# Projection stage of a decoder step: the gated channels' squares are summed before one product with ones, and that product goes ahead of k's turning

## The chip, the cores and the metric

The kernel runs on one core of a Trainium2 chip. The metric is the device time of one execution in microseconds (us); lower is better. The time of the kernel before is the median of three runs.

## The reference, cut to what matters

One decoder layer over a prompt of 2048 tokens (width 1024) and a small group of 32 sample tokens. The part that the change touches is the prompt's mixed projection and the recurrent branch:

```python
xn = rms_norm(x, p['norm_mix']) * (1 + scale1) + shift1
proj = xn @ p['w_in']
q, k, v, xr, yb = jnp.split(proj, [W_ATTN, 2 * W_ATTN, 3 * W_ATTN, 3 * W_ATTN + W_RG], axis=-1)
...
xc, conv_new = causal_conv(xr, conv_buf, p['conv_w'], p['conv_b'])
h, h_last = rg_lru(xc, h0, p['rg_wa'], p['rg_ba'], p['rg_wx'], p['rg_bx'], p['rg_lambda'])
rg = rms_norm(h * jax.nn.gelu(yb), p['norm_rg'])
```

The last line is the one that matters: for each token, the mean over the 512 gated channels of the square of h times gelu(yb), its root, and the division by it. Attention, the output projection, the routed experts and the final norm follow and are not touched.

## The kernel before, in words

The program is a series of stages, each in a block of its own with a barrier of all engines behind it: modulation, projection of the prompt (`projection_phase`), projection of the samples (`sample_projection_phase`), attention, router, experts, final norm. Everything is float32.

`projection_phase` works through the prompt in four groups of 512 tokens (`NGRP` is 4, `GRP` 512). A group's results lie with channels on the 128 partitions and tokens along the row, except v and k, whose rows are tokens (four tiles of 128 tokens, `TPG`). PSUM has eight banks of 128x512 float32, and each bank's filling is a job. `JOBS` (from L293) lists the 41 jobs of a group in order, with the engine that empties each bank: xT0 to xT7 (x turned, emptied by VectorE, DVE), xr, yb (four each, ScalarE, ACT), q (DVE), r, i (the two gates, ACT), v (ACT), k (DVE), kT (k turned, four jobs, DVE), and last rms (ACT).

TensorE (PE, L394 to L442) runs a group's jobs in that order. `free_bank` (L397) waits until the bank's last job has been emptied. Job n of a group takes bank n modulo 8, counted from 0 anew in each group. So xT0 of a group takes bank 0, which rms, job 40 of the group before, has filled: xT0 waits until ACT has emptied rms. A 128x128 transposition turns one piece (L410 for x, L439 for k), and `product` (L413, L418) accumulates matrix products into a bank. After k's last product PE waits until DVE has copied the fourth tile of k (k3) out of its bank (L435), turns k in 16 pieces, all pieces of a channel block before the next block, then waits for the squares (L441) and multiplies them by a matrix of ones, four products that add up in one bank (L442). That sums the squares over the 128 partitions and over the four channel blocks.

ACT (L445 to L503) empties xr, yb, r, i and v, takes sigmoids, exponentials and roots, normalises x of the next group (`norm`, L448), squares the gated channels (L501) once DVE has made them (L568), and takes the root of rms (L503) into `rrow`.

DVE (L506 to L577) empties xT with scale and shift (L528), finishes the group before (`finish`, L515: reciprocal of `rrow`, L518, and four multiplications, L521), does the convolution (L539, L541), copies q (L548), prepares the recurrence and scans (L563), multiplies by the gate (L568), copies k's four tiles into `k_st` (L571) and the turned k into `qk_st` (L575). In the last group `finish` follows these copies directly (L577).

SyncE (SP, L366 to L391) loads the next group's x and stores q, v, k, kT and the normed channels rgT (L380, L387) in this order, then waits until all have landed. The stage after begins when every engine has passed the barrier.

Of the kernel before, what the change touches and what calls it, by code (L numbers as in the profile page):

```python
# [11 lines left out]
ALU = mybir.AluOpType  # L12
ACT = mybir.ActivationFunctionType
AX_X = mybir.AxisListType.X

P = 128
# [84 lines left out]
def modulation_phase(nc, io, keep, sems):  # L101
# [3 lines left out]
    with ExitStack() as stack:  # L105
# [198 lines left out]
def emptied(n, engine):  # L304

    return sum(e == engine for _, e in JOBS[:n + 1])


def projection_phase(nc, io, keep, sems):
# [3 lines left out]
    with ExitStack() as stack:  # L313
# [21 lines left out]
        s_xc, s_ga, s_th, s_m2, s_m, s_sig, s_gp, s_gy, s_rg, s_rq, s_rt, s_rgn = (  # L335
            k.sem(f"p2_{n}") for n in ("xc", "ga", "th", "m2", "m", "sig", "gp", "gy", "rg", "rq", "rt", "rgn"))
        st_q, st_v, st_k, st_kT, st_rg, s_stored = (
            k.sem(f"p2_st_{n}") for n in ("q", "v", "k", "kT", "rg", "all"))
        ident, ones, vecT, modT, w_in = (keep[n] for n in ("ident", "ones", "vecT", "modT", "w_in"))
# [23 lines left out]
        with nc.Block() as block:  # L363
# [29 lines left out]
            @block.tensor  # L393
            def _(pe):  # L394
                for g in range(NGRP):

                    def free_bank(n):  # L397

                        before = [m for m in range(NJ) if m % 8 == n % 8]
                        at = before.index(n)  # L400
                        m = before[at - 1]
                        e = JOBS[m][1]
                        pe.wait_ge(out_sem[e], (g + (1 if at else 0)) * n_of[e] + emptied(m, e))
                        return bank[n % 8]

                    pe.wait_ge(s_xn, g + 1)
                    for c in range(KC):
                        ps = free_bank(JOB[f"xT{c}"])
                        for j in range(TPG):
                            mm = pe.transpose(ps[:, j * P:j * P + P], x_t[:, j, c * P:c * P + P], ident[:, :])  # L410
                        mm.then_inc(made, 1)

                    def product(name, parts):  # L413
                        ps = free_bank(JOB[name])
                        for i, (w, m) in enumerate(parts):
                            if name == "xr0":
                                wait_out(pe, f"xT{i}", g)
                            mm = pe.matmul(ps[:, :], w, m, start=(i == 0), stop=(i == len(parts) - 1))  # L418
                        mm.then_inc(made, 1)

                    for part in ("xr", "yb", "q"):
                        pe.wait_ge(sems[f"w_{part}"], 16)
                        for f in range(FC):
                            at = wcol[part] + f * P
                            product(f"{part}{f}", [(w_in[:, c, at:at + P], xnT[:, c, :]) for c in range(KC)])
                    pe.wait_ge(s_xc, g + 1)
                    for n, part in enumerate(("r", "i")):
                        for f in range(FC):
                            product(f"{part}{f}", [(keep["w_gate"][:, n, f, :], xc[:, f, :])])
                    for part in ("v", "k"):  # L430
                        pe.wait_ge(sems[f"w_{part}"], 16)
                        at = wcol[part]
                        for j in range(TPG):
                            product(f"{part}{j}", [(xnT[:, c, j * P:j * P + P], w_in[:, c, at:at + WA]) for c in range(KC)])
                    wait_out(pe, f"k{TPG - 1}", g)  # L435
                    for f in range(FC):
                        ps = free_bank(JOB[f"kT{f}"])
                        for j in range(TPG):
                            mm = pe.transpose(ps[:, j * P:j * P + P], k_st[:, j, f * P:f * P + P], ident[:, :])  # L439
                        mm.then_inc(made, 1)  # L440
                    pe.wait_ge(s_rq, g + 1)  # L441
                    product("rms", [(ones[:, :], gt[:, f, :]) for f in range(FC)])  # L442

            @block.scalar
            def _(act):  # L445
# [18 lines left out]
                for g in range(NGRP):  # L464
                    for f in range(FC):
                        wait_made(act, f"xr{f}", g)
                        act.activation(xr[:, f, CONV - 1:], bank[JOB[f"xr{f}"] % 8][:, :], ACT.Copy).then_inc(act_out, 1)
                    for f in range(FC):
                        wait_made(act, f"yb{f}", g)
                        act.activation(yb[:, f, :], bank[JOB[f"yb{f}"] % 8][:, :], ACT.Copy).then_inc(act_out, 1)  # L470
                    act.wait_ge(s_gp, g + 1)
                    act.activation(gt[:, :, :], gt[:, :, :], ACT.Sigmoid, scale=GELU_OUT).then_inc(s_sig, 1)
                    for f in range(FC):
                        wait_made(act, f"r{f}", g)
                        act.activation(ra[:, f, :], bank[JOB[f"r{f}"] % 8][:, :], ACT.Sigmoid, bias=vcol("rg_ba", f)).then_inc(act_out, 1)
                    for f in range(FC):
                        wait_made(act, f"i{f}", g)
                        act.activation(ig[:, f, :], bank[JOB[f"i{f}"] % 8][:, :], ACT.Sigmoid, bias=vcol("rg_bx", f)).then_inc(act_out, 1)
                    act.wait_ge(s_stored, g + 1)
                    act.drain()  # L480
                    for f in range(FC):
                        act.activation(th[:, f, :], ra[:, f, :], ACT.Tanh, scale=keep["coef"][:, f:f + 1])
                    act.drain()
                    for f in range(FC):
                        last = act.activation(ra[:, f, :], ra[:, f, :], ACT.Exp, scale=keep["coef"][:, f:f + 1])
                    act.drain().then_inc(s_th, 1)

                    def values(first, last):
                        for j in range(first, last):
                            wait_made(act, f"v{j}", g)  # L490
                            act.activation(v_st[:, j, :], bank[JOB[f"v{j}"] % 8][:, :], ACT.Copy).then_inc(act_out, 1)
# [11 lines left out]
                    act.activation(rrow[:, :], bank[JOB["rms"] % 8][:, :], ACT.Sqrt, bias=keep["eps"][:, 0:1]).then_inc(act_out, 1)  # L503

            @block.vector
            def _(dve):  # L506
# [18 lines left out]
                for g in range(NGRP):  # L525
                    for c in range(KC):
                        wait_made(dve, f"xT{c}", g)
                        dve.tensor_scalar(xnT[:, c, :], bank[JOB[f"xT{c}"] % 8][:, :], keep["A1T"][:, c, 0:1],  # L528
                                          modT[:, SHIFT1 + c, 0:1], ALU.mult, ALU.add).then_inc(dve_out, 1)
                    if g:  # L530
                        finish(g - 1)
# [13 lines left out]
                    dve.wait_ge(s_stored, g + 1)  # L545
                    for f in range(FC):
                        wait_made(dve, f"q{f}", g)
                        dve.tensor_copy(qk_st[:, f, :], bank[JOB[f"q{f}"] % 8][:, :]).then_inc(dve_out, 1)  # L548
# [18 lines left out]
                    dve.wait_ge(s_gy, g + 1)  # L567
                    dve.tensor_tensor(hs[:, :, :], hs[:, :, :], yb[:, :, :], ALU.mult).then_inc(s_rg, 1)  # L568
                    for j in range(TPG):
                        wait_made(dve, f"k{j}", g)  # L570
                        dve.tensor_copy(k_st[:, j, :], bank[JOB[f"k{j}"] % 8][:, :]).then_inc(dve_out, 1)  # L571
                    dve.wait_ge(st_q, 16 * g + 16)
                    for f in range(FC):
                        wait_made(dve, f"kT{f}", g)
                        dve.tensor_copy(qk_st[:, f, :], bank[JOB[f"kT{f}"] % 8][:, :]).then_inc(dve_out, 1)  # L575

                finish(NGRP - 1)  # L577

# [1618 lines left out]
```

## Time and profile before

| | |
|---|---|
| median of three runs | 2992.24 us (2990.52 to 2995.51) |
| the profiled execution's own time | 2991.91 us |
| its span in the trace | 2990.2 us |
| mean granted TensorE clock | 0.962 of full speed |
| TensorE busy | 2739.4 us, 92% of the span |
| VectorE busy | 1347.6 us, 45% |
| ScalarE busy | 963.5 us, 32% |
| GpSimd busy | 471.7 us, 16% |

Busy time of an engine says that an instruction of it was running, not that it ran at its peak. A float32 product of 128x128 by 128x512 is two records in the trace ("passes" below); a transposition is one. Row lines give the start, the length, the engine, the source line, and in brackets how long the engine sat idle before and what ended that. PEld is TensorE's loading of weights, which runs beside its products. The projection of the prompt spans from 40 us to about 674 us of the trace.

### The profile page before, as it was taken

The numbers are of one execution on the slowest core, as the hardware profiler recorded it, in microseconds if no ns is written. First come the engines' busy times: TensorE is split into PE (matmuls) and PEld (weight loads), VectorE is DVE, ScalarE is ACT, GpSimd is POOL, SyncE is SP. The second block draws the span as 40 slices with busy tenths as digits, with TensorE's granted clock in tenths as the row PEclk, the third lists the DMA queues.
The fourth block names the chain that finished last, engine by engine and source line by source line (L and its number), as shares of the span: only waits on it lengthen the run. The fifth ranks groups of instructions, "written<-read, shape, count | busy, mean of one in ns | idle before, by whom it ended". The sixth has DMA issues, their size and how long they took to land. (4 is left out here: it accounts for less than half of the span.)

```text
span 2990.2 us, 45603 instructions
## 1 busy us (share of the span) xinstructions
PE 2739.4 (92%) x15137; PEld 1363.8 (46%) x15137; DVE 1347.6 (45%) x2726; ACT 963.5 (32%) x1858; POOL 471.7 (16%) x669
## 2 busy tenths in 40 slices
PE   7999999986899898899999999399999998999978
PEld 3444444432444444444444555255555554455533
DVE  2231414132778687778786777212212221122218
ACT  2222222121777677677771221110001010010004
POOL 0101010101011111121110222211111111111123
PEclk8999999997999999999999999699999999999989
DMA  8020201018586767676664433586896479968737
GB/s 316 14 84 14 74 25 56 14 56 310 160 275 203 265 200 246 205 249 204 230 217 153 148 131 117 204 273 218 288 302 216 149 235 354 351 218 271 241 100 315
DMA packets 275921, 575.74 MB, mean 193 GB/s; under 512 B 59270, under 2 KB 75719, under 8 KB 271740
## 3 DMA queue, kind: packets, MB, share of 16 engines
q1 hardware_dynamic: 192936, 427.99, 41.4%
q0 software_dynamic: 82480, 145.43, 15.3%
q8 instruction: 89, 1.46, 0.2%
q14 instruction: 92, 0.75, 0.1%
q10 hardware_dynamic: 324, 0.10, 0.0%
HBM read 460.86 MB, written 112.29 MB: 192 GB/s over the span
## 5 line engine op out<-in xcount | busy, mean ns | idle before, releaser
L1930 PE MATMUL h<-w,xT 128*64 128x256 f32 x5120 | 589.0, 383 | 22.2 <-DMA w<-in_w 18.1
L1930 PEld LDWEIGHTS h<-w,xT 128*64 128x64 f32 x5120 | 362.7, 138 | 244.6 <-issue 75.2
L1220 DVE TENSOR_TENSOR_SCAN left<-leave,left 128x512 f32<-128x512 f32 (+3 forms) x320 | 358.7, 1121 | 159.0 <-ACT leave L1102 157.9
L418 PE MATMUL bank<-xnT,w_in 128*128 128x512 f32 x768 | 330.3, 592 | 0.0
L1943 PE MATMUL yb<-w,hT 128*64 128x512 f32 x1280 | 309.4, 604 | 0.0
L1911 ACT ACTIVATE sg<-h 128x128 f32<-128x128 f32 x160 | 44.3, 277 | 692.1 <-PE h L1930 692.1
L1023 POOL DMA_DIRECT2D w_out<-in_cache_v x256 | 137.4, 537 | 689.2 <-issue 687.6
L1589 PE MATMUL pb<-w_out,featT 128*128 128x512 f32 x512 | 227.7, 597 | 2.2 <-DVE t L1654 2.2
L418 PEld LDWEIGHTS bank<-xnT,w_in 128*128 128x128 f32 x768 | 145.6, 190 | 181.8 <-issue 180.6
L1976 DVE TENSOR_TENSOR sg<-sg,h 128x128 f32<-128x128 f32 x160 | 46.1, 288 | 388.0 <-ACT sg L1911 388.0
L418 PE MATMUL bank<-w_in,xnT 128*128 128x512 f32 x512 | 220.4, 592 | 0.0
L1271 PE MATMUL tb<-ident,take 128*128 128x128 f32 x1088 | 188.1, 289 | 23.0 <-DVE take L1126 18.4
L1102 ACT ACTIVATE leave<-zb,nbiasP 128x512 f32<-128x512 f32 (+3 forms) x320 | 203.6, 636 | 7.9 <-PE zb L1264 7.9
L1104 ACT ACTIVATE take<-zb,biasP 128x512 f32<-128x512 f32 (+3 forms) x320 | 206.1, 644 | 0.0
L1126 DVE TENSOR_TENSOR take<-take,left 128x512 f32<-128x512 f32 (+3 forms) x320 | 194.8, 609 | 15.8 <-DVE left L1220 0.4
L1271 PEld LDWEIGHTS tb<-ident,take 128*128 128x128 f32 x1088 | 117.1, 143 | 167.3 <-issue 108.6
L1258 PE MATMUL zb<-w 64*128 64x512 f32 (+3 forms) x640 | 164.4, 591 | 30.3 <-ACT take L1104 18.7
L1304 PE MATMUL tb<-ident,w_out 128*128 128x128 f32 x1024 | 159.9, 280 | 31.7 <-DMA w_out<-in_cache_k 23.2
L1291 PE MATMUL ob<-wT,vv 128*64 128x256 f32 (+1 forms) x1152 | 183.3, 398 | 1.7 <-ACT wT L1034 1.6
L1034 ACT ACTIVATE wT<-tb 128x512 f32<-128x512 f32 (+3 forms) x240 | 130.9, 545 | 102.1 <-PE tb L1271 101.1
L418 PEld LDWEIGHTS bank<-w_in,xnT 128*128 128x128 f32 x512 | 97.3, 190 | 122.5 <-issue 122.5
L1885 POOL DMA_DIRECT2D ys_d<-y x82 | 70.2, 857 | 501.3 <-DMA ys_d<-y 408.1
(372 smaller groups left out, 2873.9 us busy)
## 6 DMA issues: line engine op xcount, KB each, us to landing
w<-in_w SPq DMA_DIRECT2D x96, 2048.0 KB, 23.8
w_out<-in_cache_v POOLq DMA_DIRECT2D x256, 256.0 KB, 5.0
w_out<-in_cache_k SPq DMA_DIRECT2D x256, 256.0 KB, 3.9
ys_d<-zeros SPq DMA_DIRECT2D x32, 816.0 KB
slab<-in_w_ada SPq DMA_DIRECT2D x24, 1024.0 KB, 17.9
ys_d<-y POOLq DMA_DIRECT2D x83, 256.0 KB, 9.8
x_in<-xs_d POOLq DMA_DIRECT2D x162, 128.0 KB, 6.3
w_in<-in_w_in SPq DMA_DIRECT2D x5, 2048.0 KB, 20.3
```

The source lines that it names most:

```text
L418: mm = pe.matmul(ps[:, :], w, m, start=(i == 0), stop=(i == len(parts) - 1))
L1102: act.activation(leave[n % 4][:, 0:cols], zb[n % 3][:, 0:cols], ACT.Sigmoid, scale=-SCALE, bias=keep["nbiasP"][:, head:head + 1]).then_inc ...
L1104: act.activation(take[n % 4][:, 0:cols], zb[n % 3][:, 0:cols], ACT.Sigmoid, scale=SCALE, bias=keep["biasP"][:, head:head + 1]).then_inc(s_ ...
L1126: dve.tensor_tensor(take[n % 4][:, 0:cols], take[n % 4][:, 0:cols], left[n % 4][:, 1:cols + 1], ALU.mult).then_inc(s_w, 1)
L1220: dve.tensor_tensor_scan(left[n % 4][:, 0:cols][:, ::-1], leave[n % 4][:, 0:cols][:, ::-1], leave[n % 4][:, 0:cols][:, ::-1], left[n % 4][ ...
L1258: mm = pe.matmul(zb[(n + par) % 3][:, 0:cols], qT[pair % 2][half, t * P:t * P + P], kT[pair % 2][half, c * GRP:c * GRP + cols], start=True ...
L1271: mm = pe.transpose(to[:, j * P:j * P + P], take[n % 4][:, j * P:j * P + P], ident[:, :])
L1291: mm = pe.matmul(o[64 * par:64 * par + 64, q0:2 * P], vv[pair % 2][:, c * TPG + j, 64 * par:64 * par + 64], wT[m % 2][par][:, j, :, :].rea ...
L1304: mm = pe.transpose(to[:, i * P:i * P + P], kp[g % 2][:, i, f * P:f * P + P], ident[:, :])
L1589: mm = pe.matmul(pb[half][0:n, :], lhs, w_out[:, half, c, :], start=(c == 0), stop=(c == KC - 1))
L1930: mm = pe.matmul(h[half][q * G:q * G + G, 0:2 * P], xT[:, c % (XW // P), c // (XW // P) * G:c // (XW // P) * G + G], w13[i][:, c, :, cols] ...
L1943: mm = pe.matmul(yb[p * G:p * G + G, :], hT[:, half, q * G:q * G + G], w2[i][:, q * (EC // STRIPS) + half, p * XW:p * XW + XW], start=(hal ...
```

## The change

It has three parts. First, once DVE has copied k2 and before it copies k3, it waits for the squares and adds them up over the four channel blocks with two additions (128x1024, then 128x512); PE then makes one product with ones in place of four. Second, the job rms moves ahead of kT, so PE makes this product right behind k's products, and turns k piece by piece in the order of its tiles: all four banks of kT are claimed first, and each token tile's four pieces wait only for that tile's copy. Third, banks are counted on through the groups: the job's number over the whole stage modulo 8 names the bank, and `free_bank` waits for the job eight places before. The helper `at` gives the bank to ACT and DVE.

```diff
-        [(f"kT{f}", "dve") for f in range(FC)] + [("rms", "act")])
+        [("rms", "act")] + [(f"kT{f}", "dve") for f in range(FC)])
...
+        def at(name, g):
+
+            return bank[(g * NJ + JOB[name]) % 8]
...
-                    def free_bank(n):
-
-                        before = [m for m in range(NJ) if m % 8 == n % 8]
-                        at = before.index(n)
-                        m = before[at - 1]
-                        e = JOBS[m][1]
-                        pe.wait_ge(out_sem[e], (g + (1 if at else 0)) * n_of[e] + emptied(m, e))
-                        return bank[n % 8]
+                    def free_bank(name):
+
+                        n = g * NJ + JOB[name]
+                        if n >= 8:
+                            of, m = divmod(n - 8, NJ)
+                            e = JOBS[m][1]
+                            pe.wait_ge(out_sem[e], (of + 1) * n_of[e] + emptied(m, e))
+                        return at(name, g)
...
-                    wait_out(pe, f"k{TPG - 1}", g)
-                    for f in range(FC):
-                        ps = free_bank(JOB[f"kT{f}"])
-                        for j in range(TPG):
-                            mm = pe.transpose(ps[:, j * P:j * P + P], k_st[:, j, f * P:f * P + P], ident[:, :])
-                        mm.then_inc(made, 1)
-                    pe.wait_ge(s_rq, g + 1)
-                    product("rms", [(ones[:, :], gt[:, f, :]) for f in range(FC)])
+                    pe.wait_ge(s_sum, g + 1)
+                    product("rms", [(ones[:, :], gt[:, 0, :])])
+                    kT = [free_bank(f"kT{f}") for f in range(FC)]
+                    for j in range(TPG):
+                        wait_out(pe, f"k{j}", g)
+                        for f in range(FC):
+                            mm = pe.transpose(kT[f][:, j * P:j * P + P], k_st[:, j, f * P:f * P + P], ident[:, :])
+                            if j == TPG - 1:
+                                mm.then_inc(made, 1)
...
                     for j in range(TPG):
+                        if j == TPG - 1:
+                            dve.wait_ge(s_rq, g + 1)
+                            dve.tensor_tensor(gt[:, 0:2, :], gt[:, 0:2, :], gt[:, 2:4, :], ALU.add)
+                            dve.drain()
+                            dve.tensor_tensor(gt[:, 0, :], gt[:, 0, :], gt[:, 1, :], ALU.add).then_inc(s_sum, 1)
                         wait_made(dve, f"k{j}", g)
-                        dve.tensor_copy(k_st[:, j, :], bank[JOB[f"k{j}"] % 8][:, :]).then_inc(dve_out, 1)
+                        dve.tensor_copy(k_st[:, j, :], at(f"k{j}", g)[:, :]).then_inc(dve_out, 1)
```

The remaining lines of the diff put `at(name, g)` where a bank was named by `bank[JOB[name] % 8]`, and add the semaphore.

## Rows read from the trace of the kernel before

**Rows 1.** Busy time by stretch: us, then busy (instructions) of PE, PEld, DVE, ACT, POOL, clock, DMA.

```profile
100.00:190.00 90.00, 89.81 (x210) 39.48 (x208) 21.53 (x19) 32.00 (x40) 14.52 (x4) 1.00 0.06 23
...
200.00:345.00 145.00, 144.75 (x342) 64.04 (x339) 41.54 (x46) 36.17 (x47) 14.50 (x4) 1.00 0.10 37
```

**Rows 2.** Timeline of the joint between the first group and the second.

```profile
183.64 6.17 PE L418 MATMUL bank<-w_in,xnT 128*128 128x512 f32 x14
...
189.85 0.69 DVE L571 COPY k_st<-bank 128x512 f32<-128x512 f32 x1 [6.17 <-PE bank L418]
...
190.59 1.73 PEld L439 LDWEIGHTS bank<-ident,k_st 128*128 128x128 f32 x16 [1.61 <-DVE k_st L571]
190.59 1.97 PE L439 MATMUL bank<-ident,k_st 128*128 128x128 f32 x16 [0.78 <-DVE k_st L571]
191.36 2.48 DVE L575 COPY qk_st<-bank 128x512 f32<-128x512 f32 x4 [0.82 <-PE bank L439]
...
192.40 3.60 PE L418 MATMUL bank<-gt,ones 128*128 128x512 f32 x8
```

**Rows 3.** Timeline of the same joint, its second half, by engine (ACT, PE, DVE).

```profile
196.03 0.69 ACT L503 ACTIVATE rrow<-bank,eps 128x512 f32<-128x512 f32 x1 [19.49 <-PE bank L418]
...
196.87 3.69 PE L410 MATMUL bank<-ident,x_t 128*128 128x128 f32 x32 [0.87 <-ACT rrow L503]
200.39 15.19 PE L418 MATMUL bank<-xnT,w_in 128*128 128x512 f32 x35
...
197.53 5.84 DVE L528 TENSOR_SCALAR xnT<-bank,A1T,modT 128x512 f32<-128x512 f32 x8 [3.69 <-PE bank L410]
```

**Rows 4.** Timeline of the two later joints: k3's copy in the second and third group.

```profile
344.79 0.69 DVE L571 COPY k_st<-bank 128x512 f32<-128x512 f32 x1 [6.17 <-PE bank L418]
...
499.73 0.69 DVE L571 COPY k_st<-bank 128x512 f32<-128x512 f32 x1 [6.18 <-PE bank L418]
```

**Rows 5.** Timeline of DVE ahead of k3's copy in the first group, and of ACT.

```profile
172.31 2.29 DVE L568 TENSOR_TENSOR th<-th,yb 128x2048 f32<-128x2048 f32 x1
...
182.98 0.69 DVE L571 COPY k_st<-bank 128x512 f32<-128x512 f32 x1 [6.17 <-PE bank L418]
...
174.63 1.91 ACT L501 ACTIVATE gt<-th 128x2048 f32<-128x2048 f32 x1 [9.86 <-DVE th L568]
```

**Rows 6.** Additions and products of two tensors on DVE elsewhere, shapes apart: busy us, mean ns.

```profile
L1659 DVE TENSOR_TENSOR x<-t,x_t 128x512 f32<-128x512 f32 x32 | 22.2, 693 | 3.0
...
L1673 DVE TENSOR_TENSOR xn<-xn,rowsP 128x1024 f32<-128x1024 f32 x16 | 19.6, 1226 | 1.2
```

**Rows 7.** Timeline of the stage's end and of the next stage's start.

```profile
654.67 0.69 DVE L571 COPY k_st<-bank 128x512 f32<-128x512 f32 x1 [6.17 <-PE bank L418]
...
658.69 0.37 SPq L380 DMA_DIRECT2D kT_d<-qk_st  x1
...
661.57 3.35 DVE L518 RECIPROCAL rrow<-rrow 128x512 f32<-128x512 f32 x1 [2.91 <-ACT rrow L503]
...
667.80 0.37 SPq L387 DMA_DIRECT2D rgT_d<-th  x1
673.60 24.32 SPq L640 DMA_DIRECT2D slab<-in_w_ada  x14
```

**Rows 8.** Clock and DMA in short stretches (columns as in rows 1).

```profile
42.00:43.00 1.00, 1.00 (x7) 1.00 (x6) 0.91 (x3) 0.00 (x0) 0.00 (x0) 0.50 1.04 385
43.00:44.00 1.00, 1.00 (x7) 1.00 (x6) 0.96 (x2) 0.00 (x0) 0.00 (x0) 0.56 1.11 401
44.00:45.00 1.00, 1.00 (x11) 1.00 (x10) 1.00 (x2) 0.00 (x0) 0.00 (x0) 1.00 0.99 362
...
662.00:663.00 1.00, 0.00 (x0) 0.00 (x0) 1.00 (x1) 0.00 (x0) 0.00 (x0) 1.00 0.34 127
...
678.00:679.00 1.00, 1.00 (x12) 0.26 (x8) 0.00 (x0) 0.00 (x0) 0.11 (x1) 0.62 1.03 377
...
660.82:673.64 12.82, 0.00 (x1) 0.04 (x2) 6.10 (x6) 0.69 (x1) 0.00 (x0) 0.67 0.34 127
699.60:709.80 10.20, 9.37 (x48) 4.46 (x44) 0.69 (x1) 2.74 (x13) 0.00 (x0) 0.52 1.01 418
```

**Rows 9.** Timeline of PE at the stage's start, the first group's transpositions of x.

```profile
36.17 1.11 PE L226 MATMUL ps_f<-ident,mod_rows 128*128 128x128 f32 x4
40.07 5.54 PE L410 MATMUL bank<-ident,x_t 128*128 128x128 f32 x32 [2.79 <-ACTq L463]
```

More of the change, by code:

```diff
@@ L334, in projection_phase @@
         s_x, s_xn, s_rs, s_sq = (k.sem(f"p2_{n}") for n in ("x", "xn", "rs", "sq"))
-        s_xc, s_ga, s_th, s_m2, s_m, s_sig, s_gp, s_gy, s_rg, s_rq, s_rt, s_rgn = (
-            k.sem(f"p2_{n}") for n in ("xc", "ga", "th", "m2", "m", "sig", "gp", "gy", "rg", "rq", "rt", "rgn"))
+        s_xc, s_ga, s_th, s_m2, s_m, s_sig, s_gp, s_gy, s_rg, s_rq, s_rt, s_sum, s_rgn = (
+            k.sem(f"p2_{n}") for n in ("xc", "ga", "th", "m2", "m", "sig", "gp", "gy", "rg", "rq", "rt", "sum", "rgn"))
         st_q, st_v, st_k, st_kT, st_rg, s_stored = (
@@ L395, in _ @@
                 for g in range(NGRP):
-                    def free_bank(n):
-                        before = [m for m in range(NJ) if m % 8 == n % 8]
-                        at = before.index(n)
-                        m = before[at - 1]
-                        e = JOBS[m][1]
-                        pe.wait_ge(out_sem[e], (g + (1 if at else 0)) * n_of[e] + emptied(m, e))
-                        return bank[n % 8]
+                    def free_bank(name):
[5 more added lines that the diff above has]
+                        return at(name, g)
                     pe.wait_ge(s_xn, g + 1)
                     for c in range(KC):
-                        ps = free_bank(JOB[f"xT{c}"])
+                        ps = free_bank(f"xT{c}")
                         for j in range(TPG):
@@ L413, in product @@
                     def product(name, parts):
-                        ps = free_bank(JOB[name])
+                        ps = free_bank(name)
                         for i, (w, m) in enumerate(parts):
@@ L423, in _ @@
                         for f in range(FC):
-                            at = wcol[part] + f * P
-                            product(f"{part}{f}", [(w_in[:, c, at:at + P], xnT[:, c, :]) for c in range(KC)])
+                            of = wcol[part] + f * P
+                            product(f"{part}{f}", [(w_in[:, c, of:of + P], xnT[:, c, :]) for c in range(KC)])
                     pe.wait_ge(s_xc, g + 1)
@@ L431, in _ @@
                         pe.wait_ge(sems[f"w_{part}"], 16)
-                        at = wcol[part]
+                        of = wcol[part]
                         for j in range(TPG):
-                            product(f"{part}{j}", [(xnT[:, c, j * P:j * P + P], w_in[:, c, at:at + WA]) for c in range(KC)])
-                    wait_out(pe, f"k{TPG - 1}", g)
-                    for f in range(FC):
-                        ps = free_bank(JOB[f"kT{f}"])
-                        for j in range(TPG):
-                            mm = pe.transpose(ps[:, j * P:j * P + P], k_st[:, j, f * P:f * P + P], ident[:, :])
-                        mm.then_inc(made, 1)
-                    pe.wait_ge(s_rq, g + 1)
-                    product("rms", [(ones[:, :], gt[:, f, :]) for f in range(FC)])
+                            product(f"{part}{j}", [(xnT[:, c, j * P:j * P + P], w_in[:, c, of:of + WA]) for c in range(KC)])
+                    pe.wait_ge(s_sum, g + 1)
[7 more added lines that the diff above has]
+                                mm.then_inc(made, 1)
             @block.scalar
@@ L466, in _ @@
                         wait_made(act, f"xr{f}", g)
-                        act.activation(xr[:, f, CONV - 1:], bank[JOB[f"xr{f}"] % 8][:, :], ACT.Copy).then_inc(act_out, 1)
+                        act.activation(xr[:, f, CONV - 1:], at(f"xr{f}", g)[:, :], ACT.Copy).then_inc(act_out, 1)
                     for f in range(FC):
                         wait_made(act, f"yb{f}", g)
-                        act.activation(yb[:, f, :], bank[JOB[f"yb{f}"] % 8][:, :], ACT.Copy).then_inc(act_out, 1)
+                        act.activation(yb[:, f, :], at(f"yb{f}", g)[:, :], ACT.Copy).then_inc(act_out, 1)
                     act.wait_ge(s_gp, g + 1)
@@ L474, in _ @@
                         wait_made(act, f"r{f}", g)
-                        act.activation(ra[:, f, :], bank[JOB[f"r{f}"] % 8][:, :], ACT.Sigmoid, bias=vcol("rg_ba", f)).then_inc(act_out, 1)
+                        act.activation(ra[:, f, :], at(f"r{f}", g)[:, :], ACT.Sigmoid, bias=vcol("rg_ba", f)).then_inc(act_out, 1)
                     for f in range(FC):
                         wait_made(act, f"i{f}", g)
-                        act.activation(ig[:, f, :], bank[JOB[f"i{f}"] % 8][:, :], ACT.Sigmoid, bias=vcol("rg_bx", f)).then_inc(act_out, 1)
+                        act.activation(ig[:, f, :], at(f"i{f}", g)[:, :], ACT.Sigmoid, bias=vcol("rg_bx", f)).then_inc(act_out, 1)
                     act.wait_ge(s_stored, g + 1)
@@ L490, in values @@
                             wait_made(act, f"v{j}", g)
-                            act.activation(v_st[:, j, :], bank[JOB[f"v{j}"] % 8][:, :], ACT.Copy).then_inc(act_out, 1)
+                            act.activation(v_st[:, j, :], at(f"v{j}", g)[:, :], ACT.Copy).then_inc(act_out, 1)
                     values(0, 2)
@@ L502, in _ @@
                     wait_made(act, "rms", g)
-                    act.activation(rrow[:, :], bank[JOB["rms"] % 8][:, :], ACT.Sqrt, bias=keep["eps"][:, 0:1]).then_inc(act_out, 1)
+                    act.activation(rrow[:, :], at("rms", g)[:, :], ACT.Sqrt, bias=keep["eps"][:, 0:1]).then_inc(act_out, 1)
             @block.vector
@@ L527, in _ @@
                         wait_made(dve, f"xT{c}", g)
-                        dve.tensor_scalar(xnT[:, c, :], bank[JOB[f"xT{c}"] % 8][:, :], keep["A1T"][:, c, 0:1],
+                        dve.tensor_scalar(xnT[:, c, :], at(f"xT{c}", g)[:, :], keep["A1T"][:, c, 0:1],
                                           modT[:, SHIFT1 + c, 0:1], ALU.mult, ALU.add).then_inc(dve_out, 1)
@@ L547, in _ @@
                         wait_made(dve, f"q{f}", g)
-                        dve.tensor_copy(qk_st[:, f, :], bank[JOB[f"q{f}"] % 8][:, :]).then_inc(dve_out, 1)
+                        dve.tensor_copy(qk_st[:, f, :], at(f"q{f}", g)[:, :]).then_inc(dve_out, 1)
                     dve.wait_ge(s_th, g + 1)
@@ L574, in _ @@
                         wait_made(dve, f"kT{f}", g)
-                        dve.tensor_copy(qk_st[:, f, :], bank[JOB[f"kT{f}"] % 8][:, :]).then_inc(dve_out, 1)
+                        dve.tensor_copy(qk_st[:, f, :], at(f"kT{f}", g)[:, :]).then_inc(dve_out, 1)
                 finish(NGRP - 1)
```

## The prediction, made before the changed kernel ran

> **What bounds the kernel now.** I read first the busy time by stretch for the stage that the change touches. Between a group's start and its end TensorE is busy for 89.81 of 90 us and for 144.75 of 145, and no other engine for more than 42 [rows 1]. So inside a group TensorE alone sets the time, and a wait of another engine is free. Next I read the timeline where two groups meet, because only there PE stands still. Its last 14 passes of k's products start at 183.64 and take 6.17 us; one pass lasts 0.592, so the step from pass to pass is (6.17 - 0.592) / 13 = 0.429, the last starts at 189.22 and another could have started at 189.65 [rows 2]. It starts nothing until 190.59: it waits for DVE's copy of k3. Then come 16 transpositions in 1.81 us (to 192.40), then eight passes with ones, the last at 192.40 + 7 x 0.429 = 195.40, so that the next instruction could have started at 195.83. It starts at 196.87, after ACT's root has emptied the rms bank, and x's 32 transpositions take 3.52 us, to 200.39 [rows 3]. The joint thus takes 7.22 us from 189.65 to 196.87: 0.94 of waiting, 1.81 of turning, 3.43 of ones, 1.04 of waiting. The same copy of k3 comes at 344.79 and 499.73, 154.94 after the one before each time [rows 4], so the three joints are alike and a group is a fixed sum of PE's work.
>
> **Part one, four products become one.** PE makes two passes with ones instead of eight: 6 x 0.429 = 2.57 us less in each of the three joints, all on the path. DVE gets two additions. The trace has two-tensor operations of both shapes elsewhere, 1.226 us for 128x1024 and 0.693 for 128x512 [rows 6]; with a drain of some 0.1 that is 2.0 us. They stand between k2's copy, which ends at 183.67, and k3's, for which DVE now waits 6.17 us until 189.85 [rows 2, 5]. Their input is ready: ACT's squares end at 174.63 + 1.91 = 176.54 [rows 5]. So the sum is ready near 185.7, PE asks for it at 189.65, and DVE is back 4.1 us before k3 is made. Cost: nothing, hidden behind k3's products. Were that cover gone, 2.0 us a group would come onto the path. What is queued behind the new wait on DVE is k3's copy, and behind that kT's and the stores of k and kT on SP; the wait has been over for 7 us when DVE comes to it.
>
> **Part two, rms ahead of kT.** The two passes start at 189.65 and 190.08, and the transpositions can start at 190.51. k3's copy ends at 190.54. The pieces of k0 to k2 need nothing of it; they are 12 at 1.73 / 16 = 0.108, so the first piece of k3 starts near 191.81, 1.27 us after that copy. The wait of 0.94 is gone. What is late next is DVE: the four banks of kT are now finished together instead of one after the other. The first copy of kT started 0.77 after the first of its four transpositions, so 0.45 after the last [rows 2]; I put it at 191.81 + 0.45 = 192.26. Four copies take 2.48, to 194.74. ACT's root runs from about 190.7 to 191.4, beside the turning.
>
> **Part three, banks counted on.** xT0 to xT2 now wait for k1 to k3, xT3 for rms, xT4 to xT7 for kT0 to kT3. The first three have long been empty when x's transpositions start at 190.51 + 1.81 = 192.32. xT3 starts 12 pieces later, near 193.6, and needs the root's end at 191.4. xT4 to xT7 start near 194.1, 194.5, 195.0 and 195.4, and need the copies that end near 192.9, 193.6, 194.2 and 194.74. The margin never falls below 0.6 us. The wait of 1.04 is gone. x's transpositions end at 195.84, where xr0's first product needs the first copy of xT: DVE starts it after kT3 at about 194.8, it takes 0.8, done 195.6. That leaves 0.2 us. After that DVE makes a copy each (5.84 - 0.80) / 7 = 0.72 us [rows 3] and PE needs one each two passes, 0.86, so the margin grows. Were all four banks held up by kT's copies, the most that this could cost is their whole 2.48 us.
>
> The joint becomes 0.86 + 1.81 = 2.67 us in place of 7.22: 4.55 less, three times, **13.65 us**.
>
> **The stage's end.** Here DVE and the stores set the end. k3's copy starts at 654.67; DVE starts its reciprocal at 661.57, 6.90 later, because the root comes last; the store of rgT is issued at 667.80 and the next stage starts at 673.60 [rows 7]. Afterwards the root is done 1.5 us behind k3's product, and DVE goes into the reciprocal when its kT copies are done: 2.41 + 2.48 + 0.05 = 4.95 behind k3's copy. All that follows moves up by 6.90 - 4.95 = **1.95 us**. SP's order is kept: k's store where it was, kT's issued 0.9 later than now (4.9 in place of 4.02 behind 654.67), rgT's 1.95 earlier. kT's traffic ends now during 662 to 663 [rows 8], so it would end near 663.2 of the same scale, before rgT's issue at 665.85: they don't meet. In the other joints the same stores lie beside 145 us of PE's work and cost nothing.
>
> **The sum.** 13.65 + 1.95 = 15.6 us less than the profiled execution's own 2991.91: 2976.3. The median of the three runs is 0.33 above that execution, so I forecast **2976.5 us** for the median. Later stages start behind a barrier and move as one piece; I put their change at zero, with 2 to 3 us either way, since the three runs before spread over 5.0 us without any change.
>
> **A rule that speaks against the change.** The change puts k's 16 and x's 32 transpositions side by side, 5.3 us without a product, where now at most 3.5 us of turning stand together with a wait of 1.04 in front. What the trace shows is this: ahead of the stage PE stood still until 40.07, at the lower level of 1.2 GHz (0.50), and then ran transpositions alone [rows 9]. During 43 to 44, still within them, the granted clock began to rise, and from 44 to 45 it was 1.00 [rows 8]. So transpositions have raised the clock, and I expect them to hold it. The Trainium skill, TensorE: Matmul & The Clock Gate, Part 4 (PE-mode transpose), says that transpositions don't count as PE being busy in the same way and don't bring the full clock. By that rule the joint could fall to half speed, which is the second rival below; the trace does not agree with it.
>
> **Rivals.**
> (a) The joint keeps a wait: DVE's kT copies, now bunched, hold up xT4 or the first product. For it: only 0.2 us of margin at the first product. Against: the margins worked out above. Between 0.3 and 2.48 us a joint: 2977.4 to 2983.9; I take 2980 for the case. Chance 0.10.
> (b) The clock falls at the joints. At the next stage's start PE ran at half speed from 673.64 until about 678.6, 5 us [rows 7, 8]; half of that is lost, 2.5 us a joint, 7.5 in all: 2984.0. Against: rows 8 and 9. Chance 0.04.
> (c) A later stage gives some back. The sample projection waits for its weights' transfers, which start behind the barrier and so move with it; but attention and the experts have stretches in which clock and transfers fall differently from run to run. Up to 5 us either way on top: 2971 to 2982. Chance 0.06.
> (d) Slower than before: the clock falls in the joints and stays down. The longest stretch at half speed with PE at work is 10.2 us, 699.6 to 709.8 at 0.52 [rows 8]; that loses 5.1 us a joint, 15.3 in all, and cancels the gain (2991.6). From 5.2 us lost per joint it turns into a loss, and beyond 0.2% it needs 7.2, over 14 us at half speed behind each joint. With 20 us, 10 lost each: 2976.3 + 30 = 3006. No stretch of dense products shows this. Chance 0.01.
> (e) The change doesn't do what it says: the additions are not ready or the passes not fewer. Six passes fewer follow from the text; the squares have 7 us of slack. Were DVE's additions late by over 4 us, PE would stand still ahead of rms with all turning behind it. Each microsecond beyond costs one a joint: 2980 to 2990. Chance 0.01.
>
> **How the numbers follow.** The forecast has 0.78, its own range 2973.5 to 2979.5. About 0.2% of the time, 6 us, is what a measurement of this kernel can tell from no change, so faster means below 2986.3. Forecast, (a), (b) and (c) lie there: 0.78 + 0.10 + 0.04 + 0.06 = 0.98. I keep 0.95 for faster, 0.03 for within 0.2% and 0.02 for slower, since the later stages scatter and (b) could be dearer. The range 2972.5 to 2982.5 holds the forecast and nearly all of (a) and (c).
>
> **What would show each step.** Behind k3's last pass two passes with ones follow at once, then 16 and 32 transpositions without a gap, then xr0: 6.2 us from 189.65 to the first product instead of 10.74. DVE shows two additions of 1.2 and 0.7 us that end about 4 us before k3's copy, then a wait of about 4.1 in place of 6.17. DVE waits some 1.7 us before the first kT copy and hardly at all before x's. k3's copies stand 150.4 apart. The clock stays at 1.00 in the joints. The next stage starts 15.6 us earlier, near 658.0. The forecast is wrong if a gap over 0.3 us is left in the joint, if the granted clock shows 0.50 there, or if the span from the next stage's start to the end differs from now by more than 3 us.

## The result, and the profile after

The changed kernel's median is 2977.32 us over six runs (2973.08 to 2984.49), against 2993.61 (2990.52 to 2997.86) for the kernel before on the same chips. The ratio is 0.9947 with a 95% interval of 0.9931 to 0.9963: 16.3 us less, by medians. The forecast was 2976.5. That the two lie only 0.8 us apart is partly luck: two later medians of the same kernel are 2973.9 and 2972.2. What doesn't depend on luck is the stage's own time, read below from the trace. The profiled execution took 2973.08 us, with a span of 2971.2.

The timeline of the first joint, changed kernel:

```profile
183.16 0.69 DVE L581 COPY k_st<-bank 128x512 f32<-128x512 f32 x1 [6.18 <-PE bank L422]
183.77 1.22 DVE L577 TENSOR_TENSOR gt<-gt 128x1024 f32<-128x1024 f32 x1
185.06 0.69 DVE L579 TENSOR_TENSOR gt<-gt 128x512 f32<-128x512 f32 x1
189.83 1.02 PE L422 MATMUL bank<-gt,ones 128*128 128x512 f32 x2
190.03 0.69 DVE L581 COPY k_st<-bank 128x512 f32<-128x512 f32 x1 [4.28 <-PE bank L422]
190.69 1.91 PE L445 MATMUL bank<-ident,k_st 128*128 128x128 f32 x16
...
190.89 0.69 ACT L508 ACTIVATE rrow<-bank,eps 128x512 f32<-128x512 f32 x1 [14.16 <-PE bank L422]
...
192.38 2.48 DVE L585 COPY qk_st<-bank 128x512 f32<-128x512 f32 x4 [1.66 <-PE bank L445]
192.43 3.66 PE L414 MATMUL bank<-ident,x_t 128*128 128x128 f32 x32
194.78 5.83 DVE L533 TENSOR_SCALAR xnT<-bank,A1T,modT 128x512 f32<-128x512 f32 x8
...
195.93 7.46 PE L422 MATMUL bank<-xnT,w_in 128*128 128x512 f32 x17
```

PE has no bracket any more: two passes with ones from 189.83, k's pieces from 190.69, x's from 192.43, the first product at 195.93. That is 6.10 us from the point where k's products leave PE free to the next group's first product, in place of 10.74 [rows 2, 3]. The additions sit in DVE's old wait, of which the part behind them is left: it shrinks from 6.17 to 4.28 us. k3's copy follows its product at once, as before.

Busy time by stretch (columns as in rows 1) says the same for the later joints: PE doesn't stand still in them.

```profile
340.00:490.00 150.00, 150.00 (x386) 69.22 (x385) 48.70 (x55) 36.87 (x48) 14.53 (x4) 1.00 0.13 49
490.00:640.00 150.00, 150.00 (x387) 69.35 (x386) 48.43 (x54) 28.05 (x35) 14.52 (x4) 1.00 0.09 35
```

The timeline of the stage's end, changed kernel, to be held against [rows 7]:

```profile
640.93 0.69 DVE L581 COPY k_st<-bank 128x512 f32<-128x512 f32 x1 [4.28 <-PE bank L422]
...
643.28 2.48 DVE L585 COPY qk_st<-bank 128x512 f32<-128x512 f32 x4 [1.65 <-PE bank L445]
645.68 3.34 DVE L523 RECIPROCAL rrow<-rrow 128x512 f32<-128x512 f32 x1
645.79 0.37 SPq L384 DMA_DIRECT2D kT_d<-qk_st  x1
...
651.89 0.37 SPq L391 DMA_DIRECT2D rgT_d<-th  x1
657.71 28.99 SPq L650 DMA_DIRECT2D slab<-in_w_ada  x16
```

k3's copies now stand (640.93 - 190.03) / 3 = 150.30 us apart, against 154.94: 4.64 less for each joint. From the last such copy to the next stage it is 16.78 us instead of 18.93: 2.15 less. From the first k3 copy to the next stage, the measure used below, it went from 483.75 us to 467.68: **16.07 less**, 3 x 4.64 + 2.15. The next stage to the end took 2316.6 us before and 2313.5 in this execution, 3.1 less, which the section on the prediction comes back to.

### The profile page after: what moved, and what is told of

Same layout as the page of the kernel before. It is cut to its first block and busy times, and to the rows that moved or that the text cites. A ratio compares the mean times of both kernels' runs of the same rounds, so it can differ in the third digit from the quotient of the medians.

```text
span 2971.2 us, 45570 instructions
## 1 busy us (share of the span) xinstructions
PE 2728.3 (92%) x15113; PEld 1361.5 (46%) x15113; DVE 1355.1 (46%) x2734; ACT 964.4 (32%) x1858; POOL 475.6 (16%) x669
```

## The experiments

The whole time scatters by several us from run to run, far more than the parts to be told apart. So each experiment is read from its trace by positions within the stage: the distance between k3's copies (one group), the stretch from the last of them to the next stage's start (the stage's end), and the whole from the first k3 copy. None of them depends on when the stage began, and that turned out to be needed: the first k3 copy came anywhere from 188.24 to 190.36 us. Each of the first six experiments is a single execution. How well these positions repeat can be seen from the changed kernel, which was profiled three times: 467.68, 467.68 and 467.66 us over the whole stretch.

| kernel | distance of k3's copies | last k3 copy to next stage | first k3 copy to next stage |
|---|---|---|---|
| before | 154.94 | 18.93 | 483.75 |
| changed | 150.30 | 16.78 | 467.68 |
| four products, new order and banks | 152.88 | 19.35 | 477.98 |
| additions alone, old order and banks | 152.37 | 16.38 | 473.48 |
| changed, banks counted anew | 154.57, 152.90, 154.50 | 16.78 | 478.75 |
| changed, k turned by blocks | 150.51 | 16.00 | 467.53 |
| changed, additions behind k3's copy | 153.25 | 21.12 | 480.87 |
| changed, k turned eight times | 162.53 | 29.01 | 516.59 |
| changed, ACT copies kT | 150.30 | 13.62 | 464.52 |

### Four products in the new place

```diff
-                            dve.wait_ge(s_rq, g + 1)
-                            dve.tensor_tensor(gt[:, 0:2, :], gt[:, 0:2, :], gt[:, 2:4, :], ALU.add)
-                            dve.drain()
-                            dve.tensor_tensor(gt[:, 0, :], gt[:, 0, :], gt[:, 1, :], ALU.add).then_inc(s_sum, 1)
...
-                    pe.wait_ge(s_sum, g + 1)
-                    product("rms", [(ones[:, :], gt[:, 0, :])])
+                    pe.wait_ge(s_rq, g + 1)
+                    product("rms", [(ones[:, :], gt[:, f, :]) for f in range(FC)])
```

> The changed kernel without the two additions: rms goes ahead of kT with four products as before. Read by where the next stage (sample projection) starts, 657.71 us in the changed kernel and 673.60 before, and by the distance between k3's copies, 150.30 and 154.94. Theory (the saved passes count fully, the order alone gives only the two waits): six passes of 0.43 come back in every joint, distance 152.9, and the same 2.6 at the stage's end, next stage at 668.0. Rival (the gain is the order's; the passes with ones would lie in time in which PE waited anyway, for instance for k3's copy): distance 150.3 to 151.2, next stage below 662.

Measured: distance 152.88, next stage at 666.49; the stage had begun 1.5 us early (first k3 copy 188.51), and over the stretch it is 10.30 us more than the changed kernel, 2.58 for each of the four groups. The timeline of its first joint:

```profile
188.31 3.60 PE L422 MATMUL bank<-gt,ones 128*128 128x512 f32 x8
188.51 0.69 DVE L576 COPY k_st<-bank 128x512 f32<-128x512 f32 x1 [6.18 <-PE bank L422]
...
191.74 1.91 PE L445 MATMUL bank<-ident,k_st 128*128 128x128 f32 x16
```

The six passes lie fully on the path, and the saved passes were 10.3 of the 16.1 us. The new order and the banks alone bring the other 483.75 - 477.98 = 5.77: about 6.2 in the three joints (154.94 - 152.88 = 2.06 each), less 0.42 at the stage's end, which takes 19.35 us here and took 18.93 before. In the new order the product with ones goes first, so k's pieces and DVE's copies of kT come later, and the reciprocal stands behind them.

### The additions alone, in the kernel before

```diff
                     for j in range(TPG):
+                        if j == TPG - 1:
+                            dve.wait_ge(s_rq, g + 1)
+                            dve.tensor_tensor(gt[:, 0:2, :], gt[:, 0:2, :], gt[:, 2:4, :], ALU.add)
+                            dve.drain()
+                            dve.tensor_tensor(gt[:, 0, :], gt[:, 0, :], gt[:, 1, :], ALU.add).then_inc(s_sum, 1)
...
-                    pe.wait_ge(s_rq, g + 1)
-                    product("rms", [(ones[:, :], gt[:, f, :]) for f in range(FC)])
+                    pe.wait_ge(s_sum, g + 1)
+                    product("rms", [(ones[:, :], gt[:, 0, :])])
```

> The kernel before with the two additions and one product alone; the order kT then rms and the banks stay. Theory: 2.57 us less in each joint, distance of k3's copies 152.4, both waits (0.94 for k3's copy, 1.04 for the root) unchanged; the root at the stage's end 2.57 earlier, next stage at 663.3 to 663.5. Rival (DVE's additions cost something on the way, by k3's copy coming late): k3's copy later than its product, distance above 152.6, next stage later than 664.

Measured: distance 152.37, next stage at 663.71, which is 0.2 later than expected because the first k3 copy came 0.38 later (190.23). Both waits are still there, as the timeline of its first joint shows:

```profile
190.98 1.97 PE L439 MATMUL bank<-ident,k_st 128*128 128x128 f32 x16 [0.79 <-DVE k_st L576]
...
192.78 1.02 PE L418 MATMUL bank<-gt,ones 128*128 128x512 f32 x2
...
194.68 3.69 PE L410 MATMUL bank<-ident,x_t 128*128 128x128 f32 x32 [0.87 <-ACT rrow L503]
```

The additions with the one product are worth 10.27 us by themselves. With the 5.77 of the experiment before this makes 16.04 of the 16.07 measured: the two parts simply add up. They also divide the stage's end: the saved passes alone bring it from 18.93 to 16.38, and the new order takes back 0.40 of that.

### Banks counted anew in each group

```diff
-            return bank[(g * NJ + JOB[name]) % 8]
+            return bank[JOB[name] % 8]
...
-                        n = g * NJ + JOB[name]
-                        if n >= 8:
-                            of, m = divmod(n - 8, NJ)
-                            e = JOBS[m][1]
-                            pe.wait_ge(out_sem[e], (of + 1) * n_of[e] + emptied(m, e))
+                        n = JOB[name]
+                        same = [m for m in range(NJ) if m % 8 == n % 8]
+                        i = same.index(n)
+                        m = same[i - 1]
+                        e = JOBS[m][1]
+                        pe.wait_ge(out_sem[e], (g + (1 if i else 0)) * n_of[e] + emptied(m, e))
```

> The changed kernel, but each group counts its banks from 0 anew, so that xT0 shares a bank with kT3 of the group before. Theory: x's first transposition waits for the copy of kT3, which ends near 194.86 in the first joint in place of a start at 192.43; 2.4 to 2.6 us more in each of three joints, none at the stage's end; distance 152.8, next stage near 665.1. Rival (DVE, which copies kT and then xT, is what paces the joint anyway, so the banks don't matter): distance 150.3 to 151, next stage below 660.

Measured: 154.57, 152.90 and 154.50. Only the middle one is what was expected. The wait is there in all three, 2.41 us until kT3 is copied; what differs is the time that x's 32 transpositions take behind it. The timeline of the first, second and third joint:

```profile
194.59 5.14 PEld L415 LDWEIGHTS bank<-ident,x_t 128*128 128x128 f32 x32 [2.62 <-issue]
194.62 5.35 PE L415 MATMUL bank<-ident,x_t 128*128 128x128 f32 x32 [2.41 <-DVE qk_st L586]
...
349.15 3.48 PEld L415 LDWEIGHTS bank<-ident,x_t 128*128 128x128 f32 x32 [2.62 <-issue]
349.18 3.69 PE L415 MATMUL bank<-ident,x_t 128*128 128x128 f32 x32 [2.41 <-DVE qk_st L586]
...
502.05 5.08 PEld L415 LDWEIGHTS bank<-ident,x_t 128*128 128x128 f32 x32 [2.62 <-issue]
```

and the clock in the first joint, in half microseconds (columns as in rows 1):

```profile
194.50:195.00 0.50, 0.38 (x3) 0.41 (x4) 0.00 (x0) 0.00 (x0) 0.00 (x0) 0.78 0.00 0
195.00:195.50 0.50, 0.50 (x4) 0.50 (x3) 0.00 (x0) 0.00 (x0) 0.00 (x0) 0.50 0.19 74
...
198.50:199.00 0.50, 0.50 (x7) 0.50 (x6) 0.50 (x2) 0.00 (x0) 0.00 (x0) 1.00 0.00 0
```

In two joints of three the granted clock fell to 0.50 (1.2 GHz) as PE came out of the wait, and the transpositions took 1.6 us more until it rose. So banks that restart cost 2.6 us a joint, and 4.2 to 4.3 where the clock falls: 11.07 in all, more than two thirds of what the change brings. With 478.75 us this kernel is 5.27 slower over the stretch than the one with the additions alone (473.48), and would be 2.0 slower without the clock's fall. The reordering pays only together with the banks that count on. The other half of this question was not run: banks that count on in the old order. By the jobs' list xT0 would then share its bank with k1, and rms's bank would go to xT7, so they could remove the wait for the root without any reordering; how the 2.06 us a joint divide between order and banks is open.

### k turned by blocks

```diff
-                    for j in range(TPG):
-                        wait_out(pe, f"k{j}", g)
-                        for f in range(FC):
-                            mm = pe.transpose(kT[f][:, j * P:j * P + P], k_st[:, j, f * P:f * P + P], ident[:, :])
-                            if j == TPG - 1:
-                                mm.then_inc(made, 1)
+                    wait_out(pe, f"k{TPG - 1}", g)
+                    for f in range(FC):
+                        for j in range(TPG):
+                            mm = pe.transpose(kT[f][:, j * P:j * P + P], k_st[:, j, f * P:f * P + P], ident[:, :])
+                        mm.then_inc(made, 1)
```

> The changed kernel, but k is turned block by block after k3's copy, as before, not tile by tile. Theory (rms's two passes already cover k3's copy; the turning by pieces saves nothing more in the joints and makes kT0 later): the first transposition 0.05 to 0.1 later, distance 150.3 to 150.4; DVE's first kT copy 0.8 earlier, and with it the stage's end: next stage at 656.9 to 657.3. Rival (the pieces cover a wait): distance 151 or more, next stage at 659 or later.

Measured: distance 150.51, so 0.21 us a joint, twice the most that I had put; and at the end 16.00 instead of 16.78, since the first copy of kT starts 0.8 earlier. Over the stretch 467.53 against 467.68. The pieces cover 0.2 us of k3's copy in each joint and give it back at the stage's end. Turning by pieces is thus worth nothing in this stage (0.15 us against it); the two passes with ones in front of it do most of the covering.

### The additions behind k3's copy

```diff
                         dve.tensor_copy(k_st[:, j, :], at(f"k{j}", g)[:, :]).then_inc(dve_out, 1)
+                    dve.wait_ge(s_rq, g + 1)
+                    dve.tensor_tensor(gt[:, 0:2, :], gt[:, 0:2, :], gt[:, 2:4, :], ALU.add)
+                    dve.drain()
+                    dve.tensor_tensor(gt[:, 0, :], gt[:, 0, :], gt[:, 1, :], ALU.add).then_inc(s_sum, 1)
```

(and the same four lines taken away ahead of it)

> The changed kernel with the two additions behind k3's copy instead of ahead of it, so that nothing covers them. Theory (the additions are free only because DVE waits for k3's product): the sum is ready 2.0 us behind k3's copy, PE's product with ones starts near 192.8 in place of 189.83 in the first joint, 2.9 to 3.0 us more in each joint and at the stage's end: distance 153.3, next stage near 669.5. Rival (PE has other slack there): less than 1.5 us more a joint.

Measured: distance 153.25, 2.95 more a joint, as expected. The stage's end grew by 4.34 instead of 2.95. The timeline of the first joint and of the last group's end:

```profile
192.66 1.12 PE L422 MATMUL bank<-gt,ones 128*128 128x512 f32 x2 [2.68 <-DVE gt L580]
...
652.40 2.07 PE L422 MATMUL bank<-gt,ones 128*128 128x512 f32 x2 [2.68 <-DVE gt L580]
654.27 2.41 PE L445 MATMUL bank<-ident,k_st 128*128 128x128 f32 x16
...
656.46 2.48 DVE L584 COPY qk_st<-bank 128x512 f32<-128x512 f32 x4 [4.11 <-PE bank L445]
```

and the clock at the last group's end (columns as in rows 1):

```profile
651.50:652.00 0.50, 0.00 (x0) 0.00 (x0) 0.43 (x2) 0.00 (x0) 0.00 (x0) 0.86 0.98 381
652.00:652.50 0.50, 0.10 (x1) 0.10 (x1) 0.35 (x1) 0.00 (x0) 0.00 (x0) 0.50 1.00 389
```

In the three joints ahead of it the same wait of 2.68 us left the clock at 1.00 and the two passes took 1.12 or 1.13. At the last group's end the clock fell during the wait; the two passes took 2.07, and k's turning 2.41 instead of 1.91. DVE's first kT copy starts 4.06 us behind the product with ones there, against 2.65 in the first joint (195.31 behind 192.66). That is the missing 1.4 us.

### k turned eight times over

```diff
+                    for again in range(8):
-                    for j in range(TPG):
+                        for j in range(TPG):
...
-                            if j == TPG - 1:
+                                if j == TPG - 1 and again == 7:
```

> The changed kernel with k's 16 transpositions made eight times over in every joint, into the same banks: 14 us of transpositions alone, then x's 3.5. It tests whether a long stretch without a product lowers the granted clock. Theory (transpositions hold the clock): 1.00 throughout, each transposition still 0.108 from the next, 7 x 1.73 = 12.1 us more in each joint and at the stage's end, distance 162.4, next stage near 706. Rival (the page's rule, transpositions don't count): the granted clock shows 0.50 in the joint, transpositions 0.167 or more apart once it has fallen, and the products behind them at half speed for some microseconds: distance 166 or more, next stage 720 or later.

Measured: distance 162.53, 12.23 more; next stage at 706.92. The timeline of the first joint:

```profile
190.99 14.14 PE L446 MATMUL bank<-ident,k_st 128*128 128x128 f32 x128
...
204.96 3.66 PE L414 MATMUL bank<-ident,x_t 128*128 128x128 f32 x32
```

and the busy time of that stretch (columns as in rows 1):

```profile
190.99:208.45 17.46, 17.46 (x161) 17.46 (x160) 3.58 (x7) 0.69 (x1) 0.00 (x0) 1.00 0.17 64
```

17.46 us of transpositions without a product, and the granted clock stays at 1.00, with no transposition slower; the two later joints show the same. The Trainium skill (TensorE: Matmul & The Clock Gate, Part 4) says that transpositions don't count as busy in the same way and that the full clock doesn't engage for them. For the float32 transpositions of this kernel the run contradicts it.

### ACT copies the turned k

```diff
-        [("rms", "act")] + [(f"kT{f}", "dve") for f in range(FC)])
+        [("rms", "act")] + [(f"kT{f}", "act") for f in range(FC)])
...
                     act.activation(rrow[:, :], at("rms", g)[:, :], ACT.Sqrt, bias=keep["eps"][:, 0:1]).then_inc(act_out, 1)
+                    act.wait_ge(st_q, 16 * g + 16)
+                    for f in range(FC):
+                        wait_made(act, f"kT{f}", g)
+                        act.activation(qk_st[:, f, :], at(f"kT{f}", g)[:, :], ACT.Copy).then_inc(act_out, 1)
```

(and DVE's four copies taken away)

> The changed kernel with the four copies of the turned k made by ACT, behind its root, instead of by DVE. Theory (in the joints PE alone sets the time, at the stage's end DVE's copies stand ahead of the reciprocal): distance unchanged at 150.3; at the end DVE's reciprocal starts when the root is done, about 1.6 us behind k3's copy in place of 4.75, next stage at 654.6. Rival (the store of kT, or ACT, becomes the end): kT's store issued later than rgT's would be, next stage no earlier than 657.

Measured: distance 150.30 as in the changed kernel, so the joints don't care who copies. The timeline of its stage's end:

```profile
642.12 0.69 ACT L508 ACTIVATE rrow<-bank,eps 128x512 f32<-128x512 f32 x1 [12.39 <-PE bank L422]
642.84 3.35 DVE L527 RECIPROCAL rrow<-rrow 128x512 f32<-128x512 f32 x1 [0.89 <-ACT rrow L508]
643.60 2.06 ACT L512 ACTIVATE qk_st<-bank 128x512 f32<-128x512 f32 x4 [0.79 <-PE bank L445]
...
649.06 0.37 SPq L391 DMA_DIRECT2D rgT_d<-th  x1
654.88 2.70 SPq L650 DMA_DIRECT2D slab<-in_w_ada  x5
```

DVE goes into the reciprocal 1.58 us behind k3's copy, and the next stage starts 3.16 earlier than in the changed kernel (13.62 instead of 16.78). The rival is out: kT's store is issued at 645.69, ahead of rgT's at 649.06. The median is 2974.99 us (2972.94 to 2982.60, ratio to before 0.9952, 0.9938 to 0.9967).

### Repetitions

> The changed kernel once more, unchanged, for its scatter and as the measure beside the run before it. Next stage at 657.7 within 0.1; from there to the end 2313 to 2325 us, all scatter of the time standing in attention and behind it.

Measured: distance 150.30, next stage at 657.93; median 2973.87 us (2972.50 to 2975.39), ratio 0.9945 (0.9928 to 0.9961). From the next stage to the end it took 2312.6 us, just under the range I had put, and the next stage came 0.2 late. I had put that all scatter stands in attention and behind; that was wrong by the start of the stage, which also moves, by some 2 us in all.

> ACT's copies of the turned k once more, beside the changed kernel on the same chip, with more rounds, to see whether the 3.05 us by which the next stage starts earlier reach the whole time. Theory (later stages start behind a barrier and move as one piece, their scatter is independent): next stage at 654.9 within 0.3, median 3 us below the changed kernel's, if the scatter of 10 us from run to run lets it be seen. Rival (a later stage gives it back): next stage as early, median equal or above.

> The changed kernel as the measure beside that: next stage at 657.7 to 657.9, median between 2973 and 2978.

Measured on one chip: ACT's copies 2972.69 us (2961.84 to 2981.60, ratio 0.9935, 0.9911 to 0.9960), next stage at 654.46, and 464.52 over the stretch, the same as the first time. The changed kernel 2972.18 (2967.71 to 2979.84, ratio 0.9931, 0.9912 to 0.9949), next stage at 655.90 (a miss of 1.8 by its early start: the first k3 copy is at 188.24), 467.66 over the stretch. So ACT's copies end the stage 3.16 and 3.14 us earlier, and the whole time has not shown it: with runs of one kernel 12 to 20 us apart, a difference of 3 can't be seen in these medians. Whether a later stage gives it back stays open; the profiled executions don't decide it, as their rest, from the next stage to the end, lies between 2311.6 and 2317.4 us over all the kernels here, with the kernel before at 2316.6 and the profiled run of the change at 2313.5.

## Why the prediction was right, point by point

**The bound and the method.** TensorE alone sets a group's time, and the joints were the only place where it stood still. Taking the passes and the two waits off the joint and adding nothing for the rest gave 4.55 us a joint; it is 4.64. The two terms that came out shorter are the turning, 1.74 us without a wait in front of it where [rows 2] had given 1.81, and x's, which is 3.50 in place of 3.52. A small slip in the last sum: 2976.31 and 0.33 make 2976.6, not 2976.5.

**Part one.** Six passes, 2.57 us a joint: shown twice, by taking them back (2.58 a group) and by making them the only edit (2.57). The additions took 1.22 and 0.69 us, as the rows of other stages had it, and cost nothing where they are. The price without cover, which I had put at 2.0 us a group, was too low: with the additions behind k3's copy a joint is 2.95 longer. The step that failed there is that I priced the additions alone; what comes onto the path is the copy of k3 ahead of them too, and the handovers.

**Part two.** Both waits are gone. DVE's kT copies start 2.35 behind the start of k3's copy, where I had 2.41. My working already said that k3's copy ends with the second pass, and the run with blocks shows what follows: the pieces are worth 0.2 us a joint and nothing over the stage.

**Part three.** x's transpositions start without a wait, and xr0's first product at 195.93 with xT0's copy done at about 195.6. That margin of 0.3 us held in all joints, so rival (a) did not occur. Where the prediction was wrong is the most that a hold-up by kT's copies could cost, put at their 2.48 us a joint: with banks that restart it cost 2.60, and 4.20 to 4.27 where the clock fell.

**The stage's end.** 2.15 us for 1.95 forecast: the reciprocal starts 4.75 behind k3's copy, not 4.95. The prediction didn't ask which part brings this. The saved passes bring 2.55 and the new order costs 0.40, since the reciprocal now waits for kT's copies and no longer for the root.

**The later stages.** Put at zero with 2 to 3 us either way. The rest of the profiled runs spreads over 5.8 us among all kernels, and the three medians of the changed kernel are 2977.3, 2973.9 and 2972.2. The range given held them except the last, which lies 0.3 under it. So the scatter that I read from three runs (5.0) was too small: runs of the kernel before alone went from 2984.14 to 3001.13. The prediction also named a sign of being wrong, a span from the next stage to the end that differs from before by more than 3 us. Taken by the letter it appeared: 2313.5 and 2312.6 against 2316.6, 3.1 and 4.0 less. But the third execution of the same changed kernel has 2316.5, so this sign was set narrower than the scatter and tells nothing. The 16.3 us by medians agree with the 16.07 of the stage within an interval of about 11 to 21 us; only the trace shows the stage's part closely.

**Rivals (b) and (d), the clock.** Their mechanism, transpositions side by side that let the clock fall, is excluded by the run with k turned eight times, and the changed kernel's own joints show 1.00. Where the clock did fall, in three places of two experiments, TensorE had stood still for 2.41 or 2.68 us before, and the changed kernel has no such wait in its joints.

**Rivals (c) and (e).** No stage was shown to give anything back, but with the rest scattering over 5.8 us a few microseconds either way can't be excluded. The additions were ready 4 us ahead.

## What to carry to other kernels

Where one engine is busy for all but a few microseconds, add up its passes in the stretch where it stands still, and move work of another engine into that engine's own waits: here 1.9 us of VectorE's additions bought 2.57 of TensorE's time in each group. Count what a reordering does to the sharing of banks before trusting it, because a wait that moves by one job can cost more than the reordering saves: here counting the banks anew cost 11.07 us, and the new order with the right banks saved 5.77. And look first at which of several edits in one change carries it: here the saved passes and the loss of two waits did, and the turning by pieces did not.

## What the runs showed of the hardware that was not expected

A wait of TensorE of 2.41 us, between transpositions, let the granted clock fall to 0.50 in two joints of three, and one of 2.68 us, between products, in one of four; the two waits of the kernel before, 0.78 and 0.87 us by the same measure (the brackets), left it at 1.00. The fall cost 1.6 us behind the 2.41 us wait (x's turning 5.14 in place of 3.48) and 1.4 behind the other. So in three cases of seven such a wait had a price of its own on top of its length, which also makes two equal joints unequal. Why it fell in some and not in others is not shown. The Trainium skill (TensorE: Matmul & The Clock Gate, the table of why this matters for kernels) advises against idle gaps of more than about 3 us between bursts; here waits of 2.41 and 2.68 us were enough.
